# Column totals of the middle norms of a two-layer hybrid decoder step: one fp32 product, or two one-pass products of a split sum

## The chip, the cores and the metric

The kernel runs on one NeuronCore of one Trainium2 chip. The metric is the device time of one execution in microseconds (us); lower is better. The core has a matrix engine (TensorE, PE in the rows, whose weight loads are called PEld), VectorE (DVE), ScalarE (ACT), GpSimd (POOL) and SyncE (SP). Each works through its own list of instructions in order, and they wait for one another through semaphores.

## What is computed

The reference is one inference step of a decoder trunk with two layers, for a prompt of 1024 tokens and for 32 sample tokens (8 sequences of 4), model width 1024, MLP width 4096. Every layer has four RMS norms: ahead of the mixer and behind it, ahead of the MLP and behind it.

```python
def rmsnorm(x, g):
    xf = x.astype(jnp.float32)
    y = xf * lax.rsqrt(jnp.mean(xf * xf, -1, keepdims=True) + EPS)
    return (y * g.astype(jnp.float32)).astype(x.dtype)
...
    for l in range(DEPTH):
        gl = norm_g[l]
        h = rmsnorm(x, gl[0])
...
def squared_relu_mlp(h, w1, w2):
    return jnp.square(jax.nn.relu(h @ w1)) @ w2
```

The mixer of layer 0 is a gated DeltaNet beside a spatial gating unit, that of layer 1 an mLSTM; both lie between an input and an output projection. Everything is float32.

## The kernel before, in words

The activations stand transposed, 128 features on the partitions and tokens along a row, in 8 chunks (`KT`) of 128 features. The tokens are cut into two groups: g = 0 with 512 tokens and g = 1 with 544 (512 prompt tokens and the 32 samples). With two layers that makes 16 norms, numbered e = 0 to 15 in the table `NORMS`.

**Dense products.** A weight chunk (128 x 1024, `wst`) is split in a high part that the one-pass number format float32r can hold (`whi`, a copy on ACT, function `hi`) and the rest (`wlo`, a subtraction on DVE, function `lo`). Activations are split likewise (`hhi`, `hlo`; `h1hi`, `h1lo` in the MLP). A product is then three one-pass matmuls: high x high, low x high and high x low (`piece`, line 576). A matmul takes 512 columns for g = 0 and twice 272 for g = 1.

**Norms.** For a norm e from 2 on, ACT squares the 8 chunks one after the other into `sq2` (`square`, line 1216), and DVE adds them into `ssum` (128 partitions x 512 or 544 columns, `square`, line 1668). TensorE then adds up the 128 partitions: it multiplies `ssum`, in plain float32, by the matrix `ones`, so that every partition gets the total of its column (`norm_sum` on PE, line 647). ACT turns the totals into `rstd` with Ln and Exp (`norm_sum` on ACT, line 1240); where the table of functions in use is another one, an ACT_TABLE_LOAD goes ahead of Ln (`logs_next`, line 1081). DVE scales the chunks with `rstd` (`apply` for norms behind a mixer or MLP, `pre` for those ahead of one). Norms 0 and 1 get their sums of squares in another way, and norm 15, the last, uses five products of one column (lines 658 to 660).

**The order of the work.** One list, `PLAN.order`, is made when the program is built: pieces of dense products ("d"), and between them steps of the mixers and the norms ("sq", "on", "ap", "pr"), spread by `mix`. Each engine walks the same list and issues its own part of every item. The item ("on", e) stands among pieces of dense products that have nothing to do with norm e. PE issues the totals product there and goes on with the next piece; ACT, at the same item, issues Ln and Exp behind whatever the items ahead gave it: the evacuation of the unit that PE has just finished and the copy `whi` for the next one. All instructions of `mm` carry line 554 in the trace, all of the ACT helper `A_` line 1076.

Of the kernel before, what the change touches and what calls it, by code (L numbers as in the profile page):

```python
# [5 lines left out]
F32 = mybir.dt.float32  # L6
F32R = mybir.dt.float32r
ALU = mybir.AluOpType
ACT = mybir.ActivationFunctionType

P = 128
D = 1024
KT = D // P
# [21 lines left out]
GN = (512, 512 + NS)  # L35
G0 = (0, 512)
PARTS = (((0, 512),), ((0, 272), (272, 272)))
# [13 lines left out]
NORMS = [("pre", 0, 0, 0, "A"), ("pre", 0, 1, 0, "B"), ("post", 0, 0, 1, "A"), ("pre", 0, 0, 2, "A"),  # L51
# [258 lines left out]
def build(nc, x_prompt, x_sample, state_gdn, state_gdn_conv, state_mlstm_c, state_mlstm_n, state_mlstm_m,  # L310
# [4 lines left out]
    with ctx:  # L315
        sems = {}

        def S(name):
            if name not in sems:
                sems[name] = ctx.enter_context(nc.semaphore(name))  # L320
            return sems[name]

        def sb(name, shape, dt=F32):
            return ctx.enter_context(nc.sbuf_tensor(name, shape, dt))
# [7 lines left out]
        arena = sb("arena", [P, 12608])  # L332
        relu2 = sb("relu2", [P, 2, GN[1]])
        sq2 = sb("sq2", [P, 2, GN[1]])
        ssum = sb("ssum", [P, GN[1]])
        rstd = sb("rstd", [P, GN[1]])
        hf2 = sb("hf2", [P, 2, GN[1]])
# [1 line left out]

        ident = sb("ident", [P, P])  # L340
        ones = sb("ones", [P, P])
        maskpos = sb("maskpos", [P, P])
        masknegT = sb("masknegT", [P, P])
        maskposS = sb("maskposS", [NS, NS])
# [97 lines left out]
        DB = ctx.enter_context(nc.psum_tensor("dense", [P, 4, 512], F32))  # L442
# [109 lines left out]
        def _(pe):  # L552
# [94 lines left out]
            def norm_sum(e):  # L647
                g = NORMS[e][2]
                begin(("on", e))
                b = PLAN.jobs["on", e]["bank"]  # L650
                pe.wait_ge(S("ones_ready"), 1)
                if e < 2:
                    pe.wait_ge(S("diag"), e + 1)
                else:
                    pe.wait_ge(S("squares_added"), KT * (e - 1))
                if e == 15:

                    for t in range(4, TILES + 1):
                        _, c, n = tok(t)
                        last = mm(DB[0:n, b, t - 4:t - 3], ssum[:, c], ones[:, 0:1])  # L660
                elif g:
                    mm(DB[:, b, 0:272], ones[:, :], ssum[:, 0:272])
                    last = mm(DB[:, b + 1, 0:272], ones[:, :], ssum[:, 272:544])
                else:
                    last = mm(DB[:, b, 0:512], ones[:, :], ssum[:, 0:512])
                last.then_inc(S("job_done"), 1)
# [400 lines left out]
        def _(act):  # L1067
            steps_done, logs = [0], [True]

            def A_(out, in_, func, **how):  # L1070

                if func in (ACT.Ln, ACT.Exp):
                    logs_next()
                elif func in (ACT.Silu, ACT.Gelu, ACT.Sigmoid):
                    logs[0] = False
                return act.activation(out, in_, func, **how)  # L1076

            def logs_next():

                if not logs[0]:  # L1080
                    act.preload_act_table_set("natural_log_exp_and_others")
                    logs[0] = True
# [18 lines left out]
            def done(key):  # L1101
                act.wait_ge(S("job_done"), PLAN.jobs[key]["done"])
# [91 lines left out]
            def row_norm(e):  # L1194
                r = ssx[:, slice(*GT[e])]
                act.wait_ge(S("x_squared"), GT[e][1])
                after(own(A_(r, r, ACT.Ln, bias=epsc[:, :], scale=1.0 / D)))
                A_(r, r, ACT.Exp, scale=-0.5).then_inc(S("row_norm"), 1)

            def misc(name):  # L1200
                key = ("misc", name)
# [38 lines left out]
            def norm_sum(e):  # L1240
                g = NORMS[e][2]
                n = GN[g]
                if e:
                    act.wait_ge(S("n_stt"), KT * e)
                if e > 1:
                    logs_next()
                done(("on", e))
                if e < 2:
                    A_(like(rstd, g), out_of(("on", e), g), ACT.Copy).then_inc(S("act_evac"), 1)
                    return  # L1250
                if e == 15:
                    b = PLAN.jobs["on", e]["bank"]
                    own(A_(ssx[:, 4:8], DB[:, b, 0:4], ACT.Ln, bias=epsc[:, :], scale=1.0 / D))
                    A_(ssx[0:NS, 8:9], DB[0:NS, b, 4:5], ACT.Ln, bias=epsc[0:NS, :], scale=1.0 / D)\
                        .then_inc(S("act_evac"), 1)
                    evac_wait(act, ("on", e))
                    after(steps_done[0])
                    A_(ssx[:, 4:9], ssx[:, 4:9], ACT.Exp, scale=-0.5).then_inc(S("rstd"), 1)
                    return
                A_(like(rstd, g), out_of(("on", e), g), ACT.Ln, bias=epsc[:, :], scale=1.0 / D)\  # L1260
                    .then_inc(S("act_evac"), 1)
                evac_wait(act, ("on", e))
                A_(rstd[:, 0:n], rstd[:, 0:n], ACT.Exp, scale=-0.5).then_inc(S("rstd"), 1)
# [301 lines left out]
        def _(dve):  # L1565
            TT, STT = dve.tensor_tensor, dve.scalar_tensor_tensor
# [101 lines left out]
            def square(e, c):  # L1668
# [8 lines left out]
                    ins = TT(ssum[:, 0:n], ssum[:, 0:n], sq2[:, c % 2, 0:n], ALU.add)  # L1677
                ins.then_inc(S("squares_added"), 1)

            def row_norm(e):  # L1680

                dve.wait_ge(S("row_norm"), e + 1)
                dve.wait_ge(S("ident_ready"), 1)
                if e:
                    done(("on", 0))
                for t in range(*GT[e]):
                    _, c, n = tok(t)
                    last = dve.tensor_scalar(ssum[0:n, c], ident[0:n, 0:n], ssx[0:n, t:t + 1], None, ALU.mult)
                last.then_inc(S("diag"), 1)

            def apply(e, c):
                kind, l, g, q, name = NORMS[e]
# [430 lines left out]
            for item in PLAN.order:  # L2123
                if item == ("pr", 0, 1):
                    lo(0)
                if item[0] == "d":
                    if item[2] == 0:
                        unit_begin(item[1])
                    if item[2] == 1:
                        lo(item[1] + 1)  # L2130
                    if item[1] in PLAN.after_conv:
                        conv(item[1] - 1, item[2])
                    for key in PLAN.ends[item]:
                        unit_end(key)
                elif item[0] == "x":
                    x_in(item[1])
                elif item[0] == "misc":
                    misc(item[1])
                elif item[0] == "sq":
                    square(*item[1:])  # L2140
                elif item[0] == "rx":
                    row_norm(item[1])
                elif item[0] == "ap":
                    apply(*item[1:])
                elif item[0] == "pr":
                    pre(*item[1:])
                elif item[0] == "wgs":
                    gate_weights(item[1])
                elif item[0] == "gate2":
                    gate_turn(*item[1:])  # L2150
                elif item[0] == "gp":
                    gdn_prep(*item[1:])
                elif item[0] == "g":
                    gdn(*item[1:])
                elif item[0] == "gs":
                    gdn_sample(*item[1:])
                elif item[0] == "mp":
                    ml_prep(*item[1:])
                elif item[0] == "m":
                    ml(*item[1:])  # L2160
                elif item[0] == "ms":
                    ml_sample(*item[1:])
                elif item[0] == "y":
                    y_out(item[1])
                elif item[0] == "yx":
                    y_out(item[1], True)
                elif item[0] == "yt":
                    y_tile(*item[1:])

        @block.gpsimd  # L2170
        def _(pool):
# [8 lines left out]
            def step(ins):  # L2180
                steps_done[0] += 1
                ins.then_inc(S("const_step"), 1)
                pool.wait_ge(S("const_step"), steps_done[0])

            def start():
# [3 lines left out]
                r = rows_in  # L2189
# [3 lines left out]
                dma(r[112:113, :], gdn_norm_g).then_inc(S("rows_loaded"), 16)  # L2193
                dma(r[113:117, :], sgu_norm_g[0]).then_inc(S("rows_loaded"), 16)
                dma(r[117:119, :], mlstm_norm_g.rearrange("e (c p) -> (e c) p", p=P)).then_inc(S("rows_loaded"), 16)
                step(pool.memset(ones[:, :], 1.0))
                pool.sem_inc(S("ones_ready"), 1)
                dma(wg[:, :, :], w_in[0][0, :, GATE0:GATE0 + 2 * H].rearrange("(t p) n -> p t n", p=P))\
# [333 lines left out]
```

## Time and profile before

| | us |
|---|---|
| median of 3 runs | 2746.71 |
| lowest and highest run | 2738.3, 2747.39 |
| span of the profiled execution, first to last instruction | 2736.1 |
| PE busy in it | 2684.1 (98%) |
| PEld busy | 2393.4 (87%) |
| DVE busy | 1369.3 (50%) |
| ACT busy | 1161.7 (42%) |
| POOL busy | 217.2 (8%) |
| granted clock of TensorE, mean | 0.992 |

The profiled execution has no total of its own beside its span; the shown runs lie 2.2 to 11.3 us above it. A busy share is the time in which an engine had an instruction under way. Matmuls overlap one another, so that their mean duration is longer than the time between two starts. An idle time is put down to the instruction whose end released the engine.

### The profile page before, as it was taken

To read this page: it belongs to the slowest core of one execution; us is meant where nothing else is said; L and a number is where in the kernel's file an instruction comes from. 1 tells how busy PE (TensorE), PEld (TensorE's weight loads), DVE (VectorE), ACT (ScalarE), POOL (GpSimd) and SP (SyncE) were. 2 spreads that over 40 slices of the span, in tenths; PEclk is the share of its full clock that TensorE was granted. 3 is DMA by queue.
4 is the path that set the end of the run, shared out by engine and by line. 5 is a ranking of instruction groups with operands and counts; after the bars stand their busy time and mean duration, and the time that the engine had idled before them with its cause. 6 is when DMAs were issued, how large, how long until landed. Compare 5 with 4: busy or idle time off the path is not lost.

```text
span 2736.1 us, 40845 instructions
## 1 busy us (share of the span) xinstructions
PE 2684.1 (98%) x17050; PEld 2393.4 (87%) x17050; DVE 1369.3 (50%) x2157; ACT 1161.7 (42%) x2017; POOL 217.2 (8%) x354
## 2 busy tenths in 40 slices
PE   7999999999999999999999999999999999999998
PEld 6789888888888789889999998998877797999998
DVE  4745554645554446534443456535554447454334
ACT  5554446645454335433234235434332244333334
POOL 5110001100000000110000001110010000000000
PEclk9999999999999999999999999999999999999999
DMA  6543323623323335653333325544444334333232
GB/s 186 156 139 86 91 72 96 186 62 97 88 70 87 88 107 153 198 157 106 92 103 107 101 71 166 176 131 145 125 127 127 116 99 136 89 105 108 93 93 79
DMA packets 366567, 315.71 MB, mean 115 GB/s; under 512 B 11262, under 2 KB 339004, under 8 KB 366385
## 3 DMA queue, kind: packets, MB, share of 16 engines
q1 hardware_dynamic: 336224, 207.91, 26.2%
q0 software_dynamic: 30160, 105.20, 12.2%
q8 instruction: 135, 2.21, 0.4%
q14 instruction: 48, 0.39, 0.0%
HBM read 258.12 MB, written 54.94 MB: 114 GB/s over the span
## 4 chain that ended last, share of the span: by engine, by line
PE 81%; DVE 4%; ACT 3%; issue 1%; DMA 0%; DVEq 0%; ACTq 0%
PE dense L554 71%; PE mixer L554 9%; DVE wlo L1586 1%; ACT arena L1076 1%; ACT whi L1076 1%; PE mixer L793 0%; DVE hf L1724 0%; ACT relu L1076 0%; PE mixer L925 0%; PE mixer L997 0%; DVE hlo L1720 0%; DVE accA L1661 0%; PE mixer L946 0%; ACT h1hi L1076 0%; ACT hhi L1076 0%
## 5 line engine op out<-in xcount | busy, mean ns | idle before, releaser
L554 PE MATMUL dense<-hhi,whi 128*128 128x272 f32 (+1 forms) x3072 | 853.7, 332 | 15.0 <-DVE hlo L1720 8.8
L554 PE MATMUL dense<-hhi,wlo 128*128 128x272 f32 (+1 forms) x3072 | 827.6, 324 | 0.0
L554 PE MATMUL dense<-hlo,whi 128*128 128x272 f32 (+1 forms) x3072 | 826.3, 323 | 0.0
L1586 DVE TENSOR_TENSOR wlo<-wst,whi 128x1024 fp32r<-128x1024 f32 x384 | 469.7, 1223 | 234.8 <-ACT whi L1076 233.9
L554 PEld LDWEIGHTS dense<-hhi,whi 128*128 128x128 f32 x3072 | 516.4, 189 | 75.0 <-issue 14.8
L1076 ACT ACTIVATE whi<-wst 128x1024 fp32r<-128x1024 f32 x384 | 403.9, 1052 | 397.8 <-PE dense L554 394.2
L554 PEld LDWEIGHTS dense<-hhi,wlo 128*128 128x128 f32 x3072 | 515.1, 189 | 42.5
L554 PEld LDWEIGHTS dense<-hlo,whi 128*128 128x128 f32 x3072 | 517.6, 189 | 36.9 <-issue 0.7
L554 PE MATMUL dense<-h1hi,whi 128*128 128x272 f32 (+1 forms) x1536 | 425.0, 331 | 10.7 <-DVE wlo L1586 6.3
L554 PE MATMUL dense<-h1lo,whi 128*128 128x272 f32 (+1 forms) x1536 | 413.7, 323 | 0.0
L554 PE MATMUL dense<-h1hi,wlo 128*128 128x272 f32 (+1 forms) x1536 | 413.1, 323 | 0.0
L554 PE MATMUL mixer<-arena 128*128 128x128 f32 (+7 forms) x2000 | 296.3, 290 | 4.6 <-DVE arena L1846 2.0
L554 PEld LDWEIGHTS mixer<-arena 128*128 128x128 f32 (+4 forms) x2000 | 251.7, 177 | 47.8 <-issue 18.2
L554 PEld LDWEIGHTS dense<-h1hi,whi 128*128 128x128 f32 x1536 | 257.1, 188 | 39.5 <-DVE wlo L1586 10.0
L1602 DVE TENSOR_TENSOR h1lo<-relu,h1hi 128x544 fp32r<-128x544 f32 (+1 forms) x128 | 90.6, 708 | 372.2 <-ACT relu L1076 372.1
L554 PEld LDWEIGHTS dense<-h1hi,wlo 128*128 128x128 f32 x1536 | 256.7, 188 | 22.5
L554 PEld LDWEIGHTS dense<-h1lo,whi 128*128 128x128 f32 x1536 | 257.7, 189 | 19.8 <-issue 0.5
L1076 ACT ACTIVATE relu<-dense 128x512 f32<-128x512 f32 (+2 forms) x132 | 80.6, 610 | 392.7 <-PE dense L554 392.7
L1076 ACT ACTIVATE arena<-mixer 128x256 f32<-128x256 f32 (+7 forms) x259 | 98.2, 393 | 201.4 <-PE mixer L793 89.3
L1661 DVE TENSOR_TENSOR accA<-dense,accA 128x512 f32<-128x512 f32 (+1 forms) x168 | 116.6, 699 | 97.9 <-PE dense L554 97.5
L1677 DVE TENSOR_TENSOR ssum<-ssum,sq 128x512 f32<-128x512 f32 (+1 forms) x98 | 69.3, 707 | 127.2 <-ACT sq L1076 127.2
L1076 ACT ACTIVATE ffh<-dense 128x512 f32<-128x512 f32 (+6 forms) x124 | 62.3, 526 | 159.6 <-PE dense L554 147.1
(323 smaller groups left out, 1855.6 us busy)
## 6 DMA issues: line engine op xcount, KB each, us to landing
wst<-in_w_ff_dram SPq DMA_DIRECT2D x256, 512.0 KB, 3.9
wst<-in_w_in_even_dram SPq DMA_DIRECT2D x48, 512.0 KB, 3.9
wst<-in_w_in_odd_dram SPq DMA_DIRECT2D x48, 512.0 KB, 3.9
proj<-ffh POOLq DMA_DIRECT2D x48, 272.0 KB, 2.4
proj<-ffh POOLq DMA_DIRECT2D x48, 256.0 KB, 2.3
arena<-proj POOLq DMA_DIRECT2D x16, 512.0 KB, 4.7
wst<-in_w_out_even_dram SPq DMA_DIRECT2D x16, 512.0 KB, 4.1
arena<-proj POOLq DMA_DIRECT2D x8, 1024.0 KB, 8.0
```

Of the source, the lines that this page charges most:

```text
L554: return pe.matmul(out, lhsT, rhs, start=start, stop=stop)
L1076: return act.activation(out, in_, func, **how)
L1586: TT(wlo[:, u % 2, :], wst[:, u % 2, :], whi[:, u % 2, :].bitcast(F32), ALU.subtract)\
L1602: TT(h1lo[:, k, 0:n], r, h1hi[:, k, 0:n].bitcast(F32), ALU.subtract)\
L1661: TT(v, out_of(key, g), v, ALU.add).then_inc(S("dve_evac"), 1)
L1677: ins = TT(ssum[:, 0:n], ssum[:, 0:n], sq2[:, c % 2, 0:n], ALU.add)
```

## The change

For the 13 norms e = 2 to 14 the float32 product of `ssum` with `ones` is replaced. ACT copies `ssum` into the first half of a float32r tile `ss2`, which rounds it to what one pass can hold. DVE subtracts this from `ssum` and writes the rest into the second half. PE multiplies both halves by `onesr`, a float32r matrix of ones, and adds the two products in the same bank: 2 matmuls of 512 columns for g = 0, 4 of 272 for g = 1. `ss2` takes the place of `sq2` in memory, whose last use for this norm is over by then. Norms 0, 1 and 15 stay as they were; two semaphores get new names (`row_norm` becomes `norm_part`, `diag` becomes `norm_in`).

```diff
+        ss2 = nc.alloc_sbuf_tensor_at("ss2", [P, 2, GN[1]], F32R, offset=nc.sbuf_base - 4 * 2 * GN[1])
...
+        onesr = sb("onesr", [P, P], F32R)
...
                 pe.wait_ge(S("ones_ready"), 1)
                 if e < 2:
-                    pe.wait_ge(S("diag"), e + 1)
+                    pe.wait_ge(S("norm_in"), e + 1)
                 else:
                     pe.wait_ge(S("squares_added"), KT * (e - 1))
-                if e == 15:
+                if 1 < e < 15:
+                    pe.wait_ge(S("norm_in"), e + 1)
+                    for part in range(2):
+                        for q in range(len(PARTS[g])):
+                            last = mm(DB[:, b + q, 0:272] if g else DB[:, b, 0:512], onesr[:, :],
+                                      ss2[:, part, 272 * q:272 * (q + 1)] if g else ss2[:, part, 0:512],
+                                      start=part == 0, stop=part == 1)
+                elif e == 15:
...
                 if e > 1:
                     logs_next()
+                if 1 < e < 15:
+                    act.wait_ge(S("squares_added"), KT * (e - 1))
+                    A_(ss2[:, 0, 0:n], ssum[:, 0:n], ACT.Copy).then_inc(S("norm_part"), 1)
                 done(("on", e))
...
+            def norm_rest(e):
+
+                n = GN[NORMS[e][2]]
+                dve.wait_ge(S("norm_part"), e + 1)
+                TT(ss2[:, 1, 0:n], ssum[:, 0:n], ss2[:, 0, 0:n].bitcast(F32), ALU.subtract)\
+                    .then_inc(S("norm_in"), 1)
...
+                elif item[0] == "on":
+                    if 1 < item[1] < 15:
+                        norm_rest(item[1])
...
+                pool.memset(onesr[:, :].bitcast(F32), 1.0)
                 step(pool.memset(ones[:, :], 1.0))
```

How the instructions then stand is shown at norm 2. On ACT before; `whi` is the high part of the next weight chunk, `ffh` the evacuation of a finished unit, and the second ACT_TABLE_LOAD brings the table with Ln and Exp:

```order
L1076 ACT_TABLE_LOAD [waits job_done]
L1076 ACTIVATE ffh<-dense 128x544 [waits stored0]
L1076 ACTIVATE whi<-wst 128x1024 [waits w_loaded0,w_used]
L1081 ACT_TABLE_LOAD [waits n_stt]
L1076 ACTIVATE rstd<-dense,epsc 128x512 [waits job_done]
L1076 ACTIVATE rstd<-rstd 128x512 [waits act_evac]
```

And on ACT with the change (`ss_49` is `ss2`):

```order
L1085 ACTIVATE ffh<-dense 128x544 [waits stored0]
L1085 ACTIVATE whi<-wst 128x1024 [waits w_loaded0,w_used]
L1090 ACT_TABLE_LOAD [waits n_stt]
L1085 ACTIVATE ss_49<-ssum 128x512 [waits squares_added]
L1085 ACTIVATE rstd<-dense,epsc 128x512 [waits job_done]
L1085 ACTIVATE rstd<-rstd 128x512 [waits act_evac]
```

The copy stands behind the table load, directly ahead of Ln. On PE at the same place with the change, where the dense rows belong to an input projection:

```order
L556 MATMUL dense<-hhi,wlo 128x272 x2
L556 MATMUL dense<-ss_49,onesr 128x512 [waits squares_added,norm_in,ones_ready,act_evac]
L556 MATMUL dense<-ss_49,onesr 128x512
L556 MATMUL dense<-hhi,whi 128x272 x2
L556 MATMUL dense<-hlo,whi 128x272 x2
```

Before, one row `dense<-ssum,ones 128x512` stood there, which waited for `squares_added` and not for `norm_in`. On DVE with the change, where the `hf` row is the first that uses `rstd`:

```order
L1855 TENSOR_TENSOR arena<-ident,arena 128x2x256 [waits dve_step]
L1598 TENSOR_TENSOR wlo<-wst,whi 128x1024 [waits w_hi,dve_step]
L1696 TENSOR_TENSOR ss_49<-ssum,ss_49 128x512 [waits norm_part]
L1598 TENSOR_TENSOR wlo<-wst,whi 128x1024 [waits w_hi]
L1719 SCALAR_TENSOR_TENSOR hf<-accA,par,rstd 128x512 [waits rstd]
```

The subtraction is new between the two `wlo` rows; nothing else moved.

## Rows read from the trace of the kernel before

**Rows 1.** The page: busy time, share of the span and instructions of each engine.

```profile
PE 2684.1 (98%) x17050; PEld 2393.4 (87%) x17050; DVE 1369.3 (50%) x2157; ACT 1161.7 (42%) x2017; POOL 217.2 (8%) x354
```

**Rows 2.** Waits of PE: waiter, releaser: total us, times, longest.

```profile
PE dense L554 <- DVE wlo L1586: 12.4, 12, 2.6
...
PE dense L554 <- DVE ssum L1677: 2.2, 4, 0.7
```

**Rows 3.** Groups by form: shapes, count, busy us, mean ns, idle before.

```profile
L554 PE MATMUL dense<-ssum,ones 128*128 128x512 f32 x16 | 8.4, 606 | 3.3 <-DVE ssum L1688 2.5 <-DVE ssum L1677 0.8
L554 PE MATMUL dense<-ssum,ones 128*128 128x272 f32 x28 | 7.6, 394 | 0.7 <-DVE ssum L1677 0.7
L1076 ACT ACTIVATE hhi<-hf 128x544 fp32r<-128x544 f32 x32 | 21.0, 655 | 31.9 <-DVE hf L1724 31.7
L1076 ACT ACTIVATE hhi<-hf 128x512 fp32r<-128x512 f32 x32 | 20.1, 629 | 22.4 <-DVE hf L1724 22.2
L1677 DVE TENSOR_TENSOR ssum<-ssum,sq 128x512 f32<-128x512 f32 x49 | 33.8, 690 | 66.2 <-ACT sq L1076 66.2
```

**Rows 4.** Timeline at norm 2: start us, us, engine, line, what, [idle before].

```profile
479.75 1.05 ACT L1076 ACTIVATE whi<-wst 128x1024 fp32r<-128x1024 f32 x1
...
480.08 1.02 PE L554 MATMUL dense<-ssum,ones 128*128 128x512 f32 x2
...
480.54 0.82 PE L554 MATMUL dense<-hhi,whi 128*128 128x272 f32 x2
...
480.82 1.28 ACT L1081 ACT_TABLE_LOAD   x1
480.83 1.23 DVE L1586 TENSOR_TENSOR wlo<-wst,whi 128x1024 fp32r<-128x1024 f32 x1 [2.42 <-ACT whi L1076]
481.20 0.42 PE L554 MATMUL dense<-hlo,whi 128*128 128x272 f32 x2
...
482.11 0.69 ACT L1076 ACTIVATE rstd<-dense,epsc 128x512 f32<-128x512 f32 x1
```

**Rows 5.** Timeline at norm 10.

```profile
1707.05 1.02 PE L554 MATMUL dense<-ssum,ones 128*128 128x512 f32 x2
...
1707.95 1.28 ACT L1081 ACT_TABLE_LOAD   x1
```

**Rows 6.** Timeline at norm 4.

```profile
1027.06 1.02 PE L554 MATMUL dense<-ssum,ones 128*128 128x512 f32 x2
1027.34 0.62 ACT L1076 ACTIVATE arena<-dense 128x544 f32<-128x544 f32 x1 [2.54 <-PE dense L554]
```

**Rows 7.** Timeline at norm 8, of group 1.

```profile
1641.21 0.39 PE L554 MATMUL dense<-hhi,wlo 128*128 128x512 f32 x1
1641.43 1.08 PE L554 MATMUL dense<-ssum,ones 128*128 128x272 f32 x4
1641.63 0.60 ACT L1076 ACTIVATE arena<-dense 128x512 f32<-128x512 f32 x1 [2.58 <-PE dense L554]
...
1642.58 0.40 PE L554 MATMUL dense<-hlo,whi 128*128 128x512 f32 x1
```

**Rows 8.** Timeline at norm 5.

```profile
1056.31 0.68 DVE L1677 TENSOR_TENSOR ssum<-ssum,sq 128x512 f32<-128x512 f32 x1
...
1057.14 1.10 PE L554 MATMUL dense<-ssum,ones 128*128 128x512 f32 x2 [0.24 <-DVE ssum L1677]
```

**Rows 9.** Timeline at norm 14.

```profile
2369.97 0.72 DVE L1658 COPY arena<-dense 128x544 f32<-128x544 f32 x1 [0.56 <-PE dense L554]
...
2371.28 1.02 PE L554 MATMUL dense<-ssum,ones 128*128 128x512 f32 x2
```

**Rows 10.** Timeline of PE, two waits elsewhere in the program.

```profile
371.31 0.94 PE L554 MATMUL mixer<-arena 128*128 128x128 f32 x6 [2.02 <-DVE arena L1846]
...
2301.97 0.79 PE L554 MATMUL dense<-h1hi,whi 128*128 128x512 f32 x1 [2.12 <-DVE wlo L1586]
```

**Rows 11.** Windows: busy us (count) of PE, PEld, DVE, ACT, POOL, PEclk, DMA share, GB/s.

```profile
2301.80:2305.20 3.40, 3.23 (x8) 2.56 (x9) 2.87 (x5) 2.49 (x5) 0.00 (x0) 0.50 0.50 154
```

More of the change, by code:

```diff
@@ L1197, in row_norm @@
                 after(own(A_(r, r, ACT.Ln, bias=epsc[:, :], scale=1.0 / D)))
-                A_(r, r, ACT.Exp, scale=-0.5).then_inc(S("row_norm"), 1)
+                A_(r, r, ACT.Exp, scale=-0.5).then_inc(S("norm_part"), 1)
             def misc(name):
@@ L1678, in square @@
                 ins.then_inc(S("squares_added"), 1)
+            def norm_rest(e):
[3 more added lines that the diff above has]
+                    .then_inc(S("norm_in"), 1)
             def row_norm(e):
-                dve.wait_ge(S("row_norm"), e + 1)
+                dve.wait_ge(S("norm_part"), e + 1)
                 dve.wait_ge(S("ident_ready"), 1)
@@ L1688, in row_norm @@
                     last = dve.tensor_scalar(ssum[0:n, c], ident[0:n, 0:n], ssx[0:n, t:t + 1], None, ALU.mult)
-                last.then_inc(S("diag"), 1)
+                last.then_inc(S("norm_in"), 1)
             def apply(e, c):
```

## The prediction, made before the changed kernel ran

> **What bounds the kernel now.** I began with the page's busy shares [rows 1]: TensorE is busy for 98% of the span, DVE for 50%, ACT for 42%. So nearly every microsecond that PE spends or waits is one of the total, and work on ACT or DVE costs nothing until PE has to wait for it. The waits of PE come next [rows 2]: the largest, for the low part of the weights, is 12.4 us in 12 times, and for the sums of squares it waits 2.2 us in 4 times. The totals products thus hardly wait today: the sum is ready, or nearly, when PE gets there. The third view, the groups by form [rows 3], has the prices of the operations. The fourth, the timeline around the 13 products that change, decides, since what matters is where ACT and DVE stand when PE arrives.
>
> **The product itself (a gain).** A float32 product is recorded as two matmuls: 16 rows for the 8 products of group 0, 28 for the 7 of group 1, which has two halves [rows 3]. Its cost to the stream is read from starts, since matmuls overlap. At norm 2 the product starts at 480.08 and the second dense pair behind it at 481.20 [rows 4]. Without a product a pair of 272 columns would come about every 0.25 us, so the second pair would start at 480.33: the product costs 0.87 us. One-pass matmuls of 512 columns start 0.22 us apart (1641.21 and 1641.43 [rows 7]), so two of them cost 0.46 at most. The gain is 0.41. For group 1, at norm 8, the second dense matmul starts 1.15 after the product [rows 7] where it would start 0.23 after its place; 0.92 goes down to four times 0.125, a gain of 0.42. Thirteen times 0.415 is **5.4 us gained**.
>
> **The new chain ahead of it (a loss).** Before, PE needed only the sum. Now it needs the sum, then a copy on ACT, then a subtraction on DVE. Neither has a row of its own. For the copy the nearest rows are the copies of `hf` into `hhi`, of the same shape and formats: 0.629 us for 512 columns, 0.655 for 544 [rows 3]. For the subtraction it is the addition into `ssum`, 0.690 [rows 3], and 0.03 more for 544 columns, as the copies have it. These rows are so near that I take them as they are; were both 10% off, the sum would move by 1.7 us. The handoffs: ACT starts 0.02 after its own last instruction and DVE 0.03 after ACT's end (whi ends at 480.80, the load starts at 480.82, wlo at 480.83 [rows 4]), PE 0.15 after DVE's (sum ready at 1056.99, product at 1057.14 [rows 8]). From the moment at which ACT is free and the sum is there, the product can start 0.02 + 0.63 + 0.03 + 0.69 + 0.15 = 1.52 us later, 1.58 for group 1.
>
> ACT is not free early. It walks the same list as PE, a little behind: it evacuates the unit that PE finished just before the product, makes `whi`, and at six norms loads a table. All this lay beside PE's work while only Ln stood behind it. The copy is put behind it too, and PE, which issues in order, then waits with all its dense matmuls. Every one of the 13 places read on the timeline fits one of four kinds.
> - **Table load between the evacuation and the copy**, 3 norms (2, 6, 10). At norm 2 the load ends at 482.10 [rows 4], the product could start at 483.62, and it starts now at 480.08: 3.54 us. At norm 10 the load ends at 1709.23 and the product stood at 1707.05 [rows 5]: 3.70. Norm 6 reads 3.74. Together 11.0.
> - **Evacuation or `whi` just before**, 3 norms (4, 8, 12). At norm 4 the evacuation ends at 1027.96, product now at 1027.06 [rows 6]: 2.42. At norm 8 1642.23 against 1641.43 [rows 7]: 2.38. Norm 12, where DVE's `wlo` also comes first, reads 2.55. Together 7.4.
> - **ACT free, the sum just in time**, 4 norms (3, 5, 7, 9). At norm 5 the sum is ready at 1056.99 and PE takes it at 1057.14 [rows 8]; the copy and subtraction come between: 1.38. Norm 9 reads 1.43; at norms 3 and 7 ACT's load or free time comes 0.5 us after the sum: 1.95 and 1.15. Together 5.9.
> - **Nearly covered**, 3 norms (11, 13, 14). At norm 14 the sum is 40 us old; DVE's own copy ends at 2370.69, so the subtraction ends at 2371.40 and the product starts 0.27 after its present 2371.28 [rows 9]. With 0.66 and 0.70 for the others, 1.6.
>
> The sum of the waits is **25.9 us lost**. Ln and everything behind it is later by about the same as PE itself, so the norms' own users see no further delay. At norm 3 PE already waits for a sum that hangs on norm 2's `rstd`; that wait shrinks, and up to 1 us of the 25.9 could come back.
>
> **The clock (a loss).** A wait can cost twice. PE was idle for 2.12 us before 2301.97 [rows 10], and in the next 3.40 us the granted clock was 0.50, which is 1.2 in place of 2.4 GHz [rows 11]: 8 matmuls of 512 columns went through, 0.425 us each in place of 0.23, so that stretch cost 1.6 us. After 2.02 us idle, before 371.31 [rows 10], it did not fall. The three waits with the table load leave PE idle for about 3.4 us, beyond every idle time of this size that kept its clock, so I count 1.6 for each. The three of the second kind leave it idle for about 2.3, near both rows; I count half of the three. That is 4.5 times 1.6, **7.2 us**; the bounds are 0 and six times 1.6 = 9.6.
>
> **What costs nothing.** DVE gets 13 subtractions (9 us) and ACT 13 copies (8 us); both idle for half the span [rows 1], and while PE waits they have nothing late. On DVE, at norms 2, 6 and 10 the subtraction stands ahead of a `wlo` and holds it up, until 484.7 at norm 2 against 482.06 [rows 4]; PE needs it for its next unit, and has 36 of the 48 matmuls of the present one left behind the product, 4.5 us at 0.125, which ends past 488. If that cover were gone, each such `wlo` would cost up to 1.2 us. POOL sets one more matrix to one in the first microseconds, ahead of some small loads, and PE's first product waits for other things.
>
> **A page's rule against the row.** The first kind rests on what follows a table load. The row shows Ln starting at 482.11, 0.01 us after the load of 1.28 us ends [rows 4]. The Trainium skill (ScalarE: Activation LUTs, What ACT_TABLE_LOAD costs) gives 1.28 us for the load and about 1.38 us of drain with it, some 2.66 in all. By that rule the first kind would cost more, by an estimate from the page of 1.38 us three times, 4.1 us. The trace does not agree: no drain shows on either side of the load.
>
> **The sum.** -5.4 + 25.9 + 7.2 = +27.7 us on the profiled execution, whose span is 2736.1. Against the median of the runs, 2746.7, that gives **2774.4 us**, 1.0% slower. No change is what lies within 0.5% (13.7 us), about what a measurement of this kernel can tell.
>
> **The rivals.**
> - *The waits are given back.* PE's stop lets ACT and DVE catch up, and waits that PE has later, 12.4 us for `wlo` and the rest [rows 2], go away. Its place is the 20 us behind each norm; it decides if those waits come from a backlog that lasts. For it: PE would be no worse than its data. Against it: DVE and ACT idle half the time, so a backlog does not last, and the biggest waits lie far from the norms. With the clock untouched and 12 us back: 2746.7 - 5.4 + 25.9 - 12.4 = 2754.8, within 0.5%. Chance 0.12.
> - *The split is ready when PE comes*, so that only the gain is left. The mechanism is slack: it decides where ACT is free 1.52 us or more before the product. For it: norm 14 is nearly so [rows 9]. Against it: at norms 2, 4, 8 and 10 ACT is busy past the product's start. If it held everywhere: 2746.7 - 5.4 = 2741.3, not slower. Chance 0.04.
> - *A drain behind the table load*, as the page has it: from the rows' side, each of three copies starts later by as much as the load itself is long, 1.28: +3.8, 2778. Chance 0.03.
> - *The clock falls everywhere or nowhere.* Nowhere is +20.5, 2767.2; after all six longer waits it is +30.1, 2776.8. Both are within my own case.
>
> **How the numbers follow.** My case has 0.81, and both clock ends lie in it. The runs before span 9 us, and the median after may come from either end: 2738.3 + 20.5 = 2758.8 at the bottom; at the top 2776.8 + 1.7 for the two prices + 3.8 for the drain, and some for a `wlo` that comes late, 2786. The range is 2757 to 2786, which leaves out part of the first rival and the second. Slower by over 0.5% has 0.83 (my case and the drain, less a little at the low end), within 0.5% 0.15, faster 0.02.
>
> **What would show it.** Right: PE waits for DVE at line 1696 twelve or thirteen times, about 25 us in total, longest 3.4 or so; the waits for the sum itself are gone; ACT idles less before Ln than now; stretches at half clock follow norms 2, 6 and 10; the one-pass products take 0.46 to 0.5 us of the stream. Wrong: waits there under 10 us in sum, or waits as forecast with PE's idle total less than 15 us above today's, which would mean that they are given back.

## The result, and the profile after

The change makes the kernel slower. Its runs have a median of 2767.39 us (2765.57 to 2773.9, 4 runs), the kernel before 2742.51 us beside them (2738.12 to 2747.39, 4 runs): ratio 1.0087, 95% interval 1.0070 to 1.0104, so 24 us by the ratio and 24.9 by the medians. Run again in a later round, it came out the same (1.0088, in the experiments). One run further down, at 2897.7 us and a clock of 0.881, belongs to a slower state of the chip and is in none of the means and ratios. The forecast was +27.7 us and 2774.4, in a range from 2757 to 2786.

| | before, us | after, us |
|---|---|---|
| profiled execution, total | not listed | 2767.51 |
| its span | 2736.1 | 2765.5 |
| PE busy | 2684.1 | 2688.4 |
| span less PE busy | 52.0 | 77.1 |

PE's idle time is longer by 25.1 us, its busy time by 4.3. These are two single executions, 29.4 us apart in span, more than the runs are: the one of the kernel before had a mean clock of 0.992, where its runs have 0.990 on average. DVE and ACT have 8 us more work each. The line of the page that answers to [rows 1]:

```profile
PE 2688.4 (97%) x17050; PEld 2398.6 (87%) x17050; DVE 1377.7 (50%) x2170; ACT 1169.9 (42%) x2030; POOL 217.9 (8%) x355
```

The waits of PE in the changed kernel, as in [rows 2]: who waited for whom, total us, times, longest.

```profile
PE dense L556 <- DVE ss L1696: 25.3, 12, 3.6
PE dense L556 <- DVE wlo L1598: 12.5, 11, 2.6
...
PE dense L556 <- DVE ssum L1689: 0.6, 1, 0.6
```

The first row is new, and it alone is as large as the growth of the idle time. (1.5 us of it were waits for the sum before; the row for the sum has shrunk to 0.6.) Line 1696 is the subtraction that makes the rest of the sum (`ss` is `ss2`). The waits for the weights' low part are what they were.

The groups by form give the prices that the forecast took from neighbours [rows 3]. The copy measures 0.627 and 0.652 us, the subtraction 0.691 and 0.722:

```profile
L1696 DVE TENSOR_TENSOR ss<-ssum,ss 128x512 fp32r<-128x512 f32 x7 | 4.8, 691 | 11.9 <-ACT ss L1085 11.6
...
L1085 ACT ACTIVATE ss<-ssum 128x512 fp32r<-128x512 f32 x7 | 4.4, 627 | 2.1 <-DVE ssum L1689 2.0
...
L1696 DVE TENSOR_TENSOR ss<-ssum,ss 128x544 fp32r<-128x544 f32 x6 | 4.3, 722 | 6.7 <-ACT ss L1085 6.5
...
L1085 ACT ACTIVATE ss<-ssum 128x544 fp32r<-128x544 f32 x6 | 3.9, 652 | 2.9 <-DVE ssum L1689 2.9
```

The timeline at norm 2 of the changed kernel, to be held beside [rows 4] (start us, us, engine, line, what, [idle before]):

```profile
483.36 1.05 ACT L1085 ACTIVATE whi<-wst 128x1024 fp32r<-128x1024 f32 x1
483.43 0.41 PE L556 MATMUL dense<-hhi,wlo 128*128 128x272 f32 x2
...
484.43 1.28 ACT L1090 ACT_TABLE_LOAD   x1
...
485.72 0.63 ACT L1085 ACTIVATE ss<-ssum 128x512 fp32r<-128x512 f32 x1
486.38 0.69 DVE L1696 TENSOR_TENSOR ss<-ssum,ss 128x512 fp32r<-128x512 f32 x1 [4.36 <-ACT ss L1085]
486.99 1.22 DVE L1598 TENSOR_TENSOR wlo<-wst,whi 128x1024 fp32r<-128x1024 f32 x1
487.22 1.09 PE L556 MATMUL dense<-ss,onesr 128*128 128x512 f32 x2 [3.38 <-DVE ss L1696]
```

ACT makes `whi`, loads the table, copies; DVE subtracts; PE stands still all the while. The last dense pair starts at 483.43, so the product would have started at 483.68 and starts at 487.22: 3.54 us, the figure forecast. Norm 4, where an evacuation alone stands ahead of the copy [rows 6]:

```profile
1038.33 0.41 PE L556 MATMUL dense<-hhi,wlo 128*128 128x272 f32 x2
1038.86 0.62 ACT L1085 ACTIVATE arena<-dense 128x544 f32<-128x544 f32 x1 [2.53 <-PE dense L556]
1039.38 0.62 ACT L1085 ACTIVATE ss<-ssum 128x512 fp32r<-128x512 f32 x1
1040.04 0.69 DVE L1696 TENSOR_TENSOR ss<-ssum,ss 128x512 fp32r<-128x512 f32 x1 [2.45 <-ACT ss L1085]
...
1040.88 0.70 PE L556 MATMUL dense<-ss,onesr 128*128 128x512 f32 x2 [2.13 <-DVE ss L1696]
```

2.30 us against 2.42 forecast; ACT overlaps the copy with the evacuation by 0.1. Norm 5, where the sum comes just in time [rows 8]:

```profile
1069.53 0.68 DVE L1689 TENSOR_TENSOR ssum<-ssum,sq 128x512 f32<-128x512 f32 x1
...
1070.31 0.63 ACT L1085 ACTIVATE ss<-ssum 128x512 fp32r<-128x512 f32 x1 [2.04 <-DVE ssum L1689]
1070.97 0.69 DVE L1696 TENSOR_TENSOR ss<-ssum,ss 128x512 fp32r<-128x512 f32 x1 [0.76 <-ACT ss L1085]
...
1071.81 0.71 PE L556 MATMUL dense<-ss,onesr 128*128 128x512 f32 x2 [1.67 <-DVE ss L1696]
```

Here ACT itself waited for the sum. PE is idle for 1.67 us, 0.24 before: 1.43 more, 1.38 forecast. At norm 14 the product starts 0.16 late where 0.27 was forecast.

**The clock.** In the profile of after, stretches at half clock follow norms 2, 3, 6, 8, 9 and 10. I call the start of such a stretch a fall. The window behind norm 2 shows what one costs (busy us and count of PE, PEld, DVE, ACT, POOL, then PEclk, DMA share and GB/s):

```profile
487.30:490.70 3.40, 3.40 (x14) 3.21 (x15) 1.77 (x3) 1.32 (x2) 0.00 (x0) 0.50 0.92 311
```

Fourteen matmuls where 26 go through at full clock (the same window of a run shown below). The second profile of the same kernel (`change_again`) has falls behind the same six norms. Norms 4 and 12, idle for 2.13 and 2.29 us, are followed by none in either, and the 2.12 us wait of [rows 10], elsewhere in the program, was not followed by a fall this time. The first matmuls after that wait are at full clock:

```profile
2331.97 0.50 PE L556 MATMUL dense<-h1hi,whi 128*128 128x512 f32 x1 [2.12 <-DVE wlo L1598]
2332.31 0.39 PE L556 MATMUL dense<-h1lo,whi 128*128 128x512 f32 x1
```

### The profile page after: what moved, and what is told of

The parts are those of the page before. It is cut to its first block, busy times and chain, and to the rows that moved or that the text cites. A ratio compares the mean times of both kernels' runs of the same rounds, so it can differ in the third digit from the quotient of the medians.

```text
span 2765.5 us, 40881 instructions
## 1 busy us (share of the span) xinstructions
PE 2688.4 (97%) x17050; PEld 2398.6 (87%) x17050; DVE 1377.7 (50%) x2170; ACT 1169.9 (42%) x2030; POOL 217.9 (8%) x355
## 4 chain that ended last, share of the span: by engine, by line
PE 82%; DVE 3%; ACT 3%; issue 1%; DMA 0%; DVEq 0%; ACTq 0%
PE dense L556 71%; PE mixer L556 9%; DVE wlo L1598 1%; ACT arena L1085 1%; ACT whi L1085 1%; PE mixer L802 0%; ACT relu L1085 0%; ACT L1090 0%; DVE ss L1696 0%; PE mixer L934 0%; PE mixer L1006 0%; ACT h1hi L1085 0%; DVE accA L1673 0%; ACT ss L1085 0%; ACT hhi L1085 0%
## 5 line engine op out<-in xcount | busy, mean ns | idle before, releaser
L556 PEld LDWEIGHTS dense<-h1hi,wlo 128*128 128x128 f32 x1536 | 256.3, 188 | 22.2
L556 PEld LDWEIGHTS dense<-h1lo,whi 128*128 128x128 f32 x1536 | 257.3, 188 | 19.7 <-issue 0.5
```

Source lines behind the costliest of these rows:

```text
L556: return pe.matmul(out, lhsT, rhs, start=start, stop=stop)
```

## The experiments

My theory after the first comparison: the loss is the chain copy, subtraction, product, and what makes it long is where the copy stands in ACT's list; the products themselves gain. Open was how much of the 24 us is clock. All variants are edits of the changed kernel. Ratios are to the kernel before on the same chip, with 95% intervals. Since the result lists the mean granted clock of every run, a second figure can be read: the mean of time times clock, which takes the scatter of the clock out (an estimate, as if all work scaled with the clock; it has no interval).

| run | runs | us, mean | clock, mean | ratio to before | time x clock, less that of before |
|---|---|---|---|---|---|
| split_on_dve | 11 | 2746.4 | 0.9911 | 0.9998 (0.9988 to 1.0008) | +3.1 |
| copy_ahead_of_load | 5 | 2763.4 | 0.9898 | 1.0056 (1.0044 to 1.0068) | +16.4 |
| fp32_behind_the_chain | 4 | 2781.1 | 0.9865 | 1.0120 (1.0106 to 1.0135) | +24.8 |
| kept_busy | 6 | 2768.5 | 0.9897 | 1.0073 (1.0060 to 1.0085) | +21.1 |
| change_again | 6 | 2770.3 | 0.9893 | 1.0088 (1.0074 to 1.0103) | +22.2 |
| rounded_sum_two_products | 12 | 2741.5 | 0.9906 | 0.9982 (0.9971 to 0.9993) | -2.8 |
| rounded_sum_one_product | 12 | 2738.0 | 0.9910 | 0.9970 (0.9960 to 0.9980) | -5.2 |
| only_norms_2_6_10 | 6 | 2757.8 | 0.9890 | 1.0043 (1.0027 to 1.0058) | +9.0 |
| split_on_dve_with_slack | 12 | 2745.7 | 0.9902 | 1.0000 (0.9988 to 1.0013) | -0.2 |
| fp32_behind_the_chain_again | 5 | 2780.2 | 0.9870 | 1.0130 (1.0107 to 1.0153) | +25.2 |

The kernel before had means of 2746.9 us at 0.9898, 2746.2 at 0.9899 and 2745.2 at 0.9904 in the three groups of runs (the first 4, the next 4 and the last 2 rows; 17, 23 and 17 runs).

**The split made on DVE, early.**

```diff
-                if 1 < e < 15:
-                    act.wait_ge(S("squares_added"), KT * (e - 1))
-                    A_(ss2[:, 0, 0:n], ssum[:, 0:n], ACT.Copy).then_inc(S("norm_part"), 1)
...
+                if c == KT - 1 and e < 15:
+                    norm_split(e)
...
-            def norm_rest(e):
+            def norm_split(e):
...
-                dve.wait_ge(S("norm_part"), e + 1)
+                dve.wait_ge(S("squares_added"), KT * (e - 1))
+                link(dve.tensor_copy(ss2[:, 0, 0:n], ssum[:, 0:n]))
```

> Both steps of the split are made by VectorE right behind the last addition into the sum, so that no copy stands in ScalarE's list; TensorE's two one-pass products stay as in the change. My theory (the copy's place behind ScalarE's evacuation, weight copy and table load makes the waits): the waits for the rest of the sum fall from 25.3 us to about 6, all at norms where the sum comes just in time (1.3 us each at 3, 5 and 9, 0.9 at 6, less at 7, 10, 11, 13), no half-clock stretch follows a norm, and the time is that of the kernel before within 3 us. Rival (one-pass products of a split sum cost PE the time whatever makes the split, or VectorE's 1.2 us more per norm hold up the weights): waits for the weights' low part grow by 5 us or more, or the time stays 10 us or more above before.

The time fell to that of the kernel before, and the waits to 5.4 us in 4 times, with the same products and the same arithmetic. No half-clock stretch follows a norm:

```profile
PE dense L556 <- DVE wlo L1595: 13.4, 12, 2.4
...
PE dense L556 <- DVE ss L1696: 5.4, 4, 2.0
```

So the loss came with the copy's place in ACT's list, not with the products. The time is flattered by a clock of 0.9911, above the 0.9898 of before; with the clock taken out the run is 3.1 us above, and the starts on the trace say 2: products late by 5.2, shorter by 4.4, and 1.2 as follows. The wait for the weights' low part grew by only 1.0 us, not the 5 of the rival, but it grew at one place that can be named: just ahead of norm 2, DVE has mixer work queued before a `wlo`, and the early split goes ahead of it all. Timeline of DVE and PE there:

```profile
477.23 0.43 DVE L1695 CAST ss<-ssum 128x512 fp32r<-128x512 f32 x1
477.69 0.69 DVE L1696 TENSOR_TENSOR ss<-ssum,ss 128x512 fp32r<-128x512 f32 x1
478.30 1.12 DVE L1845 SCALAR_TENSOR_TENSOR arena<-mixer,cols,arena 128x128 f32<-128x128 f32 x4
...
481.98 1.23 DVE L1595 TENSOR_TENSOR wlo<-wst,whi 128x1024 fp32r<-128x1024 f32 x1
...
483.26 0.52 PE L556 MATMUL dense<-hhi,whi 128*128 128x272 f32 x2 [1.79 <-DVE wlo L1595]
```

The same matmul waited 0.62 us in the kernel before: 1.17 us more, the length of copy and subtraction.

**The copy ahead of the table load.** The three lines of ACT's copy are moved ahead of the wait for `n_stt` and of `logs_next()`, nothing else.

> The changed kernel with ScalarE's copy issued ahead of its wait for the previous users and of the table load, nothing else moved. My theory: the three norms with a load between evacuation and copy wait 1.3 us less each (2: 3.5 to 2.2, 6: 3.7 to 2.4, 10: 3.7 to 2.4), the others 0.3 us less in sum, so the waits for the rest fall from 25.3 to about 21; if the clock then still falls after them the time is 4 us under the change, if it does not up to 9 under. Rival (the load is paid in any case, since Ln comes behind it): norms 2, 6 and 10 wait as before and the time does not move.

The waits for the rest fell by 5 us to 20.3, the time by 7 to 9 us against the change; what is beyond the 5 is clock or scatter. At norm 2 the load now lies beside the subtraction:

```profile
486.91 0.62 ACT L1085 ACTIVATE ss<-ssum 128x512 fp32r<-128x512 f32 x1
487.55 1.28 ACT L1090 ACT_TABLE_LOAD   x1
487.56 0.69 DVE L1696 TENSOR_TENSOR ss<-ssum,ss 128x512 fp32r<-128x512 f32 x1 [2.94 <-ACT ss L1085]
...
488.40 0.98 PE L556 MATMUL dense<-ss,onesr 128*128 128x512 f32 x2 [1.96 <-DVE ss L1696]
```

1.96 us idle in place of 3.38. A half-clock stretch still follows norms 2, 3 and 8 in this profile, none norms 6 and 10.

**The chain with the old product.** PE waits for the split and then multiplies the unsplit sum:

```diff
                 if 1 < e < 15:
                     pe.wait_ge(S("norm_in"), e + 1)
-                    for part in range(2):
...
-                elif e == 15:
+                if e == 15:
```

> The copy and the subtraction are made and waited for as in the change, but TensorE multiplies the unsplit sum in float32 as before (the split is left unused). My theory: the waits stay at 25 us, and the products give back what the one-pass form gained, 4 to 5.4 us, so the time is that much above the change. Rival (the one-pass form gains nothing, since a float32 product overlaps its neighbours): the time equals the change's within 1.5 us.

> The run with the chain and the float32 products once more. Its first four runs had a mean clock of 0.9865 against 0.9895 of the change, worth 8 us, and nothing in my theory says that a float32 product costs clock. If that was the scatter of the clock's falls, the clock is now 0.988 to 0.990 and the time about 5 us above the change, ratio 1.0105. If float32 products behind an idle wait do cost clock, it is 0.987 or less again and the ratio 1.012 or more.

The waits are those of the change to the tenth (25.3 us, 12 times, longest 3.6). Time times clock is 2.6 and 3.0 us above that of the change, less than the 4 to 5.4 expected for the one-pass form. The time itself is 10 us above, though, and in both rounds, on two chips: the clock is 0.9865 and 0.9870 on the mean of 9 runs, against 0.9893 to 0.9895 in the 10 runs of the change. Two other variants on the chip of the first round have 0.9897 and 0.9898, so it is not the chip. Of the nine runs three have the 0.990 of the change, at 2773 to 2776 us, and six have 0.984 to 0.987. I had put the first of these down as possible scatter, and the second round speaks against that. One such place, norm 6, where the four records of the product take 2.15 us at half clock:

```profile
1119.18 2.15 PE L556 MATMUL dense<-ssum,ones 128*128 128x272 f32 x4 [3.57 <-DVE ss L1691]
```

Why this variant loses more clock stays open. Its profile of the first round has 18 falls between 60 and 2740 us where both profiles of the change have 10, but only 6 of them behind norms, as in the change; others, at 791, 876 and 931 us for instance, are far from any changed product. So it isn't shown that the falls come from the float32 products behind their waits.

**PE kept busy while it waits.**

```diff
                 pe.wait_ge(S("ones_ready"), 1)
+                for _ in range({2: 28, 3: 20, 4: 17, 6: 29, 8: 17, 9: 18, 10: 29, 12: 19}.get(e, 0)):
+                    mm(DB[:, b, 0:P], onesr[:, :], onesr[:, :])
```

> The changed kernel, with one-pass products of 128 columns of ones with ones (17 to 29 of them, results overwritten) put into the product's own bank ahead of TensorE's wait at the eight norms with the longest waits. My theory (an idle wait costs a second time through the clock): the products start at the same times, no half-clock stretch follows a norm (6 did in the change's profile), and the time falls by up to 9 us, 1.6 for each stretch avoided. Rival (the clock's falls after norms replace falls that would have come anyway elsewhere, so they cost nothing net): the time stays within 2 us of the change, or half-clock stretches appear in other places in like number.

Norm 2's product starts at 487.22, as in the change, and the window behind it is at full clock, 26 matmuls in place of 14:

```profile
483.69 3.24 PE L556 MATMUL dense<-onesr 128*128 128x128 f32 x28
...
487.22 0.71 PE L556 MATMUL dense<-ss,onesr 128*128 128x512 f32 x2 [0.30 <-DVE ss L1698]
```

```profile
487.30:490.70 3.40, 3.40 (x26) 3.31 (x27) 2.15 (x3) 1.32 (x2) 0.00 (x0) 1.00 0.93 309
```

No fall follows any of the norms, and yet the mean clock of the runs, 0.9897, is hardly above the change's, and the ratio 1.0073 is 4 us under it with intervals that overlap. In this profile PE was at half clock at 606, 698, 790, 875 and 930 us and eleven other places, the start and the end of the program among them, in stretches where nothing was changed. Between 60 and 2740 us these are 13 falls, none behind a norm, against 10 with 6 behind norms in the change. My 9 us did not come; the rival, that falls avoided behind norms turn up elsewhere, fits better, but 4 us of difference can't be excluded.

**The change once more, and one kind of norm alone.** The edit of the second run is a list `SPLIT = [2, 6, 10]` in place of the condition `1 < e < 15`, with the semaphores counted by place in the list.

> The changed kernel once more, on the chip of the runs beside it. If the clock's falls behind the norms add to the others (my term of 7 us), its runs have a mean granted clock 0.002 to 0.003 below those of the kernel before and the difference is about 27 us. If they come in place of falls elsewhere, the mean clock is within 0.001 of before and the difference is 20 to 22 us, the waits of 25 less the products' 5.

> The change applied to norms 2, 6 and 10 alone, those with a table load ahead of the copy; the others keep their float32 product of the unsplit sum. My theory (each norm costs its own wait, by where ScalarE stands): three waits of 3.5 to 3.8 us, 11 in sum, less 1.2 for the products, so 9.8 us above before if the clock adds nothing and up to 14.6 if it falls three times more; ratio 1.0035 to 1.005. Rival (waits of early norms are made good by fewer waits later, or the norms depend on one another): the three waits are not those of the full change, or the time is under 5 us above before.

The change had a mean clock 0.0006 below before, worth 1.6 us, and came out 24.1 us slower: by its clock the case without a clock term, by its time between the two. The three norms alone wait 10.5 us in 3 times, 3.37, 3.57 and 3.53 idle, as in the full change, and cost 11.6 us in the mean; the norms do not depend on one another.

```profile
PE dense L557 <- DVE ss L1697: 10.5, 3, 3.6
```

**The products without the chain.** The last addition writes the rounded sum, so ACT and DVE have nothing extra; the low part of the sum is left out.

```diff
-                    ins = TT(ssum[:, 0:n], ssum[:, 0:n], sq2[:, c % 2, 0:n], ALU.add)
+                    total = ss2[:, 0, 0:n] if c == KT - 1 and e < 15 else ssum[:, 0:n]
+                    ins = TT(total, ssum[:, 0:n], sq2[:, c % 2, 0:n], ALU.add)
```

> No split at all: the last addition writes the sum rounded to float32r, TensorE multiplies this same half twice in one pass each, and Ln scales by half (the low part of the sum is left out). It has the change's TensorE work without its chain. My theory: no wait for a rest, PE waits for the sum as the kernel before does (2 us), and the time is 3 to 5.4 us under before, ratio 0.998 to 0.999. Rival (one-pass products gain nothing by themselves): ratio 1.000.

> As the run beside it, but only one product of the rounded sum, scaled as before (the low part of the sum is left out). My theory: another 0.22 us for each of 13 norms, 3 us more, so 6 to 8.5 us under before, ratio about 0.9975. Rival (something else than stream time on TensorE sets the cost of a product): equal to the run with two products.

Both came as expected: 0.9982 and 0.9970, so 4.7 and 8.2 us less than before in the mean. The one-pass form does gain. At norm 14 with two products the second dense pair starts 0.71 us after the product (2370.47 and 2371.18), where it was 1.10 before (2371.28 and 2372.38): 0.39 gained. At norm 4 nothing is gained, because the next dense matmul then waits for the evacuation of its bank:

```profile
1031.20 0.62 PE L556 MATMUL dense<-ss,onesr 128*128 128x512 f32 x2
1031.48 0.62 ACT L1084 ACTIVATE arena<-dense 128x544 f32<-128x544 f32 x1 [2.54 <-PE dense L556]
...
1032.25 0.49 PE L556 MATMUL dense<-hhi,whi 128*128 128x272 f32 x2 [0.43 <-ACT arena L1084]
```

**An exact version with slack only.** As the first experiment, with `SPLIT = [2, 8, 11, 12, 13, 14]`.

> The split on VectorE right behind the last addition, only for norms 2, 8, 11, 12, 13 and 14, whose sum is there early enough; 3, 4, 5, 6, 7, 9 and 10 keep the float32 product. Left out are the norms where the sum comes just in time, and 4 and 10, whose next dense matmul waits for an evacuation in any case. My theory: no wait for a rest over 0.2 us, 0.3 to 0.4 us gained at each of the six, 2 to 2.4 us in sum, ratio 0.999 (hardly clear of no change). Rival (VectorE's 1.2 us per split hold up the weights): waits for the weights' low part grow, ratio 1.000 or above.

Ratio 1.0000 (0.9988 to 1.0013): neither my 2 us nor a loss can be told. The profile has what both theories said, products shorter by 0.34 to 0.42 us at the six norms, 2.4 in sum, and the matmul ahead of norm 2 again idle for 1.79 us, 1.2 more than before. What is left of the gain, 1.2 us, is below what these runs can tell. Of the versions tried, only the two that drop the low part of the sum are clearly faster than the kernel before; no exact one is.

## Why the prediction was right, and where it was not

**Where the wait arises, and its size: right.** Forecast 25.9 us, the trace has 25.3 in 12 waits, longest 3.6 against 3.4 or so. The forecast counted from starts; counted so, the 13 products are late by 25.4 us: 10.9 for the first kind (forecast 11.0), 7.0 for the second (7.4), 6.0 for the third (5.9) and 1.4 for the fourth (1.6). Norm 2 has 3.54 (3.54), 4 has 2.30 (2.42), 5 has 1.43 (1.38) and 14 has 0.16 (0.27), forecast in brackets. Two runs show that it is the place in ACT's list and not the amount of work: the copy put ahead of the load shortened the three waits by 1.4 us each, and the copy put on another engine, with the same two operations per norm, took most of them away.

**The prices of copy and subtraction: right**, within 1%, since the rows beside them had the same shapes and formats.

**The gain of the products: about right.** Forecast 5.4, the two-product run shows 4.7 us in time (2.8 with the clock taken out). The step that took 0.41 for every norm was too even: at norms 4 and 10 the next dense matmul waits for a bank, and the product is hidden. In the changed kernel itself the wait covers that evacuation, so norms 4 and 10 gain too (0.6 each), and the 13 starts show about 5.0 us, read at full clock.

**The clock: the term that was mis-sized.** I counted 4.5 stretches of 1.6 us, 7.2 us, on top. The count was too low: six norms are followed by a fall in both profiles of the change, among them 3 and 9, for which I had counted none though they wait 2.51 and 2.23 us, while 4 and 12 have none. What such a fall adds was too high. The mean clock of the repeated change is below that of before by 0.0006 only, 1.6 us. Waits and products alone make 20.3 us (25.3 - 5.0), so the whole difference of 24 leaves about 4, of which 1.6 is this clock and the rest is not accounted for. The error was to price a fall behind a wait as one more, where a fall may come in place of another; the mean clocks and the run with PE kept busy speak for that, and no run shows how it comes about. A count by profile is too rough to tell: 10 falls between 60 and 2740 us with the change, but 5, 7, 7, 10 and 10 in the profiles of five kernels whose longest such wait is 2.0 us, the kernel before with 5 the lowest. The term brought the forecast to 27.7 in place of about 24, inside its range.

**One sign was wrong.** I wrote that ACT would idle less before Ln than now. It idles more, 25.0 us in place of 19.7. Rows of Ln before (line 1076) and after (line 1085), with the idle time behind the bar:

```profile
L1076 ACT ACTIVATE rstd<-dense,epsc 128x512 f32<-128x512 f32 x7 | 4.8, 689 | 10.4 <-PE dense L554 10.4
L1076 ACT ACTIVATE rstd<-dense,epsc 128x544 f32<-128x544 f32 x6 | 4.3, 714 | 9.3 <-PE dense L554 9.3
L1085 ACT ACTIVATE rstd<-dense,epsc 128x512 f32<-128x512 f32 x7 | 4.8, 690 | 14.0 <-PE dense L556 14.0
L1085 ACT ACTIVATE rstd<-dense,epsc 128x544 f32<-128x544 f32 x6 | 4.3, 716 | 11.0 <-PE dense L556 11.0
```

I had seen that ACT would no longer be early where it was, as at norm 14, and missed that the new chain starts on ACT itself: behind its copy it now waits at every norm for DVE's subtraction and PE's product, 1.6 to 3.5 us each. At norm 2 it did not wait at all before, and now idles for 2.0 us there. This cost PE nothing.

**The rivals.** Waits given back: no. The waits for `wlo` are 12.5 us after and 12.4 before, and norm 3, where I allowed for up to 1 us back, waits its full 1.94 more (2.51 against 0.57 idle). Split ready in time: only at norm 14, nearly. The drain behind a table load: the copy starts at 485.72, 0.01 after the load's end, so the time that the Trainium skill (ScalarE: Activation LUTs, What ACT_TABLE_LOAD costs) gives for a drain does not show at this place either. The `wlo` behind the subtraction cost nothing at norms 2, 6 and 10, as said.

## What to carry to other kernels

When a step is put ahead of an engine that sets the time, ask first where the helper engine stands at that moment, not how busy it is: ACT was idle for 58% of the span and still late for 10 of the 13 copies, because it follows PE by an evacuation, a weight copy or a table load. At the other three (norms 5, 9 and 13) it waited for the sum itself. A product made 0.4 us shorter is no bargain if its operand then needs two more steps, on two other engines, that nothing covers. If such a step is wanted, issue it where its input is finished, on the engine that finishes it, and then look at what it is now ahead of there.

## What the runs showed of the hardware that I had not expected

- The clock falls in part at places that change from run to run in a program that does not change. Both profiles of the change have falls behind norms 2, 3, 6, 8, 9 and 10, but elsewhere one has them at 108, 211, 324 and 528 us and the other at 273, 406, 525 and 607. Each stretch moves all that follows by about 1.5 us (an estimate from the 12 matmuls of 0.125 us that are missing in the window above). The runs of the kernel before lie from 2740.3 to 2751.0 us on one chip, and over those 17 runs the time falls as the mean clock rises (correlation -0.84). A difference of 5 us needs many runs, or the clock beside them.
- The variant with float32 products behind the waits had a lower mean clock, 0.9865 and 0.9870, than the one with one-pass products behind the same waits, 0.9893 to 0.9895: about 7 us. It was seen on two chips and is not explained.
